# Delta rule's recurrence with heads in pairs on 128 partitions and block diagonal states

## The chip, the cores and the metric

One core of a Trainium2 chip runs the kernel. The metric is the device time of one execution in microseconds (us), the median of some runs. The engines: PE (TensorE: matmul; PEld is its load of weights), DVE (VectorE), ACT (ScalarE), POOL (GpSimd), SP (SyncE, which issues DMAs). All data are fp32, and a matmul of fp32 leaves two records in the trace, a transposition one.

## What is computed

Two layers of a first block (attention, gated MLP, convolution, feed-forward on 512 tokens and 256 context tokens), and one layer of a second block. The change touches only the second block's delta rule: 6 heads of 64 columns, 512 tokens in 8 chunks of C = 64. The reference of that part:

```python
def gated_delta_rule(q, k, v, beta, g):
    ...
    L = jnp.where(strict, jnp.einsum('bhncd,bhnsd->bhncs', k_beta, k) * decay, 0.0)
    A = jnp.eye(C, dtype=f32) + L
    u = lax.linalg.triangular_solve(A, v * beta[..., None], left_side=True, lower=True, unit_diagonal=True)
    w = lax.linalg.triangular_solve(A, k_beta * jnp.exp(gc)[..., None], left_side=True, lower=True, unit_diagonal=True)
    qk = jnp.einsum('bhncd,bhnsd->bhncs', q, k) * decay
    q_dec = q * jnp.exp(gc)[..., None]
    k_dec = k * jnp.exp(gc[..., -1:] - gc)[..., None]
    g_last = jnp.exp(gc[..., -1])

    def step(S, xs):
        u_i, w_i, qk_i, qd_i, kd_i, gl_i = xs
        v_new = u_i - jnp.einsum('bhcd,bhde->bhce', w_i, S)
        o = jnp.einsum('bhcd,bhde->bhce', qd_i, S) + jnp.einsum('bhcs,bhse->bhce', qk_i, v_new)
        S = S * gl_i[..., None, None] + jnp.einsum('bhcd,bhce->bhde', kd_i, v_new)
        return S, o
```

Behind it stand a sparse attention of 6 heads, a pooling branch, an output projection and a feed-forward layer.

## The kernel before

The program is written out by hand for each engine: `second_pe`, `second_act`, `second_dve` and `second_pool` are the instruction streams of the second block, and semaphores (`signal`, `.at`, `wait_ge`, `then_inc`) order them. Each engine works its stream in program order. `Chain` orders dependent instructions on one engine: `link` waits for the instruction itself, `note` only counts it, `meet` waits for all counted so far. `bank(b, n, at)` is a slice of one of the eight banks of PSUM. `turn` is a transposition by PE. In `pe.matmul(out, a, b)` the first operand a is the stationary one: the trace writes its rows\*columns first (64\*64) and then the moving operand's or the output's shape. Where an operand has 64 partitions, PE works in half of its rows; where the output has 64 partitions, in half of its columns.

Tokens lie in four tiles of 128 (i = 0..3), so a tile holds two chunks: an even one in the partitions 0 to 63, an odd one in 64 to 127 (the slice r). A unit u is three heads of one tile, so there are 8 units. The stages, in order of time:

- Stage A (L1004 to L1007, evictions L831): `heads_cm(g)` turns q and k, one head at a time, from token-major to channel-major, [64 partitions, 512 tokens]: 12 groups of 4 transpositions into `qT` and `kT`, through four banks.
- Decay products (L1009 to L1023): for each of 24 heads and tiles, four matmuls of 128\*128 (L1017, L1018) form exponents, and two of 64\*128 (L1020, L1021) form k k' and k q'. ScalarE takes six exponentials per unit, VectorE multiplies (L1320, L1323).
- Transpositions of L (L1025), then VectorE forms the first inverses (L1335), and a third group of `heads_cm` turns the decayed q (L1032): 6 groups of 4.
- Inverse levels (L1035 to L1073): 5 levels of 8 units, with ScalarE and VectorE; the second form of the inverse is had by a transposition.
- w and u products (L1077 to L1088): per head one matmul of 128\*64 (L1084, w, channel-major in 64 partitions) and one of 128\*128 with 64 moving columns (L1086, u). ScalarE evicts w into `kT`, VectorE u into `qkv2` (L1371). Then VectorE clears `state` (L1373).
- Recurrence (PE L1092 to L1111, ACT L883, DVE L1374 to L1386), 8 chunks one after another. PE waits for the state (s_s_up), multiplies it by w (L1097, 6 matmuls), VectorE subtracts from u (L1379), PE forms for each head the state's increment (L1105), q times state (L1107) and the intra-chunk part (L1109), all 64\*64 with 64 moving columns. Then VectorE scales the state (L1382), adds the increment (L1384), and adds the two parts of the output (L1386), after ScalarE has evicted q times state.
- Behind the recurrence: 13 groups of transpositions for the sparse attention (L1116), VectorE's additions (L1397), a matmul with loaded weights (L1129).

Beside the recurrence GpSimd multiplies gains into the attention's q and k (L776 to L783) once the w and u products are done.

## Time and profile before

| | us |
|---|---|
| median of 3 runs | 4323.83 |
| lowest, highest | 4321.07, 4327.37 |
| the profiled execution | 4320.28 |
| its span | 4318.3 |

The profiled execution's clock was on average 0.964 of full speed. The page's busy times are shares of the whole span. The table of stages gives for each stretch the span, the busy time and number of records of each engine, and behind them PEclk, the granted clock of TensorE: 1.00 is 2.4 GHz, 0.50 is 1.2 GHz. In the chain each line is the piece that the end of the program goes back to: start, length, what. In a timeline a line with xN holds N records in a row; its length runs from the first one's start to the last one's end, and the bracket gives the idle time before it and who ended it. Records on PE overlap: the distance from one start to the next tells the pace.

### The profile page before, as it was taken

What the parts mean: (1) busy time and instruction counts of PE and PEld (TensorE: products, weight loads), DVE (VectorE), ACT (ScalarE), POOL (GpSimd) and SP (SyncE); (2) the same over time, 40 slices, a digit from 0 to 9 for tenths busy, and PEclk for the clock granted to TensorE, in tenths of its full rate; (3) what the DMA queues carried; (4) which work ended last, traced back from release to release, by engine and by line L of the source; (5) the groups of instructions that cost most, each with busy time, mean ns of one, the idle gap of its engine ahead of it and who ended that gap; (6) DMA issues with size and microseconds to landing.
All of it is one profiled execution on the core that took longest, in us unless ns stands there. A gap on an engine that the chain in (4) does not pass through costs nothing.

```text
span 4318.3 us, 36448 instructions
## 1 busy us (share of the span) xinstructions
PE 4046.4 (94%) x13693; PEld 2274.7 (53%) x13693; DVE 2026.2 (47%) x3719; ACT 884.8 (20%) x1767; POOL 389.8 (9%) x252
## 2 busy tenths in 40 slices
PE   6999989999998999998998999989998968599999
PEld 3344555555554554544445444446664457556665
DVE  2030530898013456565324099136666135455666
ACT  2111520000123111113133000221112044242111
POOL 1110000254121000000000034110000000000000
PEclk8999999999999999999999999999999989599999
DMA  5552001111112111111110222222222200102222
GB/s 210 195 196 76 2 5 59 59 39 59 39 39 83 44 59 59 59 59 61 59 59 5 72 71 72 78 88 80 96 78 75 73 24 12 49 1 78 98 78 78
DMA packets 124950, 294.51 MB, mean 68 GB/s; under 512 B 5130, under 2 KB 13370, under 8 KB 124800
## 3 DMA queue, kind: packets, MB, share of 16 engines
q1 hardware_dynamic: 107824, 236.58, 15.5%
q0 software_dynamic: 16976, 55.84, 3.8%
q8 instruction: 105, 1.72, 0.2%
q14 instruction: 45, 0.37, 0.0%
HBM read 290.23 MB, written 2.18 MB: 68 GB/s over the span
## 4 chain that ended last, share of the span: by engine, by line
PE 87%; DVE 6%; ACT 3%; DMA 2%; issue 1%; POOL 0%; DVEq 0%; SPq 0%; ACTq 0%
PE psum L357 30%; PE psum L1944 30%; PE psum L2003 14%; PE psum L1938 3%; PE psum L2048 2%; DMA sb_rc<-in_ada_b 1%; PE psum L2031 1%; ACT sb_rc L1703 1%; PE psum L1989 1%; DMA sb_ring<-in_ada_w 1%; PE psum L1043 1%; ACT sb_rb L1703 1%; PE psum L1063 1%; PE psum L2032 1%; ACT sb_ht L1703 0%
## 5 line engine op out<-in xcount | busy, mean ns | idle before, releaser
L1944 PE MATMUL psum<-sb_ht,sb_ring 128*128 128x512 f32 (+1 forms) x2448 | 891.7, 526 | 3.7 <-DVE sb_kvt L2331 2.1
L1944 PEld LDWEIGHTS psum<-sb_ht,sb_ring 128*128 128x128 f32 x2448 | 464.0, 190 | 431.2 <-issue 409.8
L2319 DVE SCALAR_TENSOR_TENSOR sb_rc<-sb_rc,sb_vec x960 | 475.6, 573 | 0.0
L2003 PE MATMUL psum<-sb_ring,sb_ht 128*128 128x512 f32 (+1 forms) x1088 | 464.4, 588 | 5.1 <-DVE sb_rc L2363 3.5
L1703 ACT ACTIVATE sb_rc<-psum 128x512 f32<-128x512 f32 (+2 forms) x330 | 167.1, 524 | 1160.4 <-DVE sb_ra L519 308.1
L357 PE MATMUL psum<-sb_ring,sb_rc 128*128 128x512 f32 x868 | 391.8, 593 | 7.5 <-DVE sb_rc L503 7.5
L2003 PEld LDWEIGHTS psum<-sb_ring,sb_ht 128*128 128x128 f32 x1088 | 207.6, 192 | 260.9 <-issue 255.7
L357 PE MATMUL psum<-sb_ht,sb_ring 128*128 128x256 f32 (+1 forms) x1152 | 305.9, 415 | 0.0
L1703 ACT ACTIVATE sb_kvt<-psum 128x512 f32<-128x512 f32 (+2 forms) x197 | 99.8, 533 | 950.4 <-PE psum L1944 788.1
L1944 PE MATMUL psum<-sb_rc,sb_ring 128*128 128x512 f32 (+1 forms) x768 | 276.6, 522 | 4.3 <-ACT sb_rc L1703 2.5
L357 PEld LDWEIGHTS psum<-sb_ring,sb_rc 128*128 128x128 f32 x868 | 164.5, 190 | 216.6 <-issue 204.2
L357 PE MATMUL psum<-sb_rb,sb_rc 128*128 128x512 f32 x588 | 268.3, 592 | 0.0
L357 PEld LDWEIGHTS psum<-sb_ht,sb_ring 128*128 128x128 f32 x1152 | 219.7, 191 | 71.5 <-issue 0.9
L1703 ACT ACTIVATE sb_rc<-sb_rc 128x512 f32<-128x512 f32 (+3 forms) x232 | 143.1, 686 | 536.0 <-DVE sb_rc L488 526.2
L1944 PEld LDWEIGHTS psum<-sb_rc,sb_ring 128*128 128x128 f32 x768 | 145.6, 190 | 134.8 <-issue 124.5
L357 PE MATMUL psum<-sb_kvt,sb_rc 128*128 128x256 f32 (+1 forms) x672 | 189.0, 426 | 9.4 <-DVE sb_kvt L438 9.4
L1938 PE MATMUL psum<-sb_ident,sb_rb 128*128 128x128 f32 (+3 forms) x748 | 116.4, 298 | 83.0 <-ACT sb_rb L1703 18.7
L357 PEld LDWEIGHTS psum<-sb_rb,sb_rc 128*128 128x128 f32 x588 | 111.7, 190 | 133.2 <-issue 130.6
L1663 POOL TENSOR_TENSOR sb_rb<-sb_kvt 128x768 f32<-128x768 f32 (+1 forms) x16 | 127.5, 7980 | 441.1 <-ACT sb_kvt L1703 441.1
L357 PEld LDWEIGHTS psum<-sb_kvt,sb_rc 128*128 128x128 f32 x672 | 130.6, 195 | 59.5 <-issue 20.9
L1938 PEld LDWEIGHTS psum<-sb_ident,sb_rb 128*128 128x128 f32 (+3 forms) x748 | 88.8, 149 | 126.4 <-issue 49.6
L2003 PE MATMUL psum<-sb_ring,sb_rb 128*128 128x512 f32 x320 | 140.5, 600 | 8.2 <-issue 8.2
(355 smaller groups left out, 4399.9 us busy)
## 6 DMA issues: line engine op xcount, KB each, us to landing
sb_ring<-in_w_in SPq DMA_DIRECT2D x37, 2048.0 KB, 7.9
sb_ring<-in_w_ff SPq DMA_DIRECT2D x32, 2048.0 KB, 7.9
sb_rc<-in_ada_w POOLq DMA_DIRECT2D x20, 2048.0 KB, 8.3
sb_ring<-in_w_ffn SPq DMA_DIRECT2D x16, 2048.0 KB, 7.9
sb_ring<-in_w_out SPq DMA_DIRECT2D x6, 2048.0 KB, 8.0
sb_ring<-in_ada_w SPq DMA_DIRECT2D x4, 2048.0 KB, 12.8
sb_ring<-in_w_gmlp_o SPq DMA_DIRECT2D x4, 2048.0 KB, 8.3
sb_ring<-in_w_attn_o SPq DMA_DIRECT2D x4, 2048.0 KB, 8.0
```

The lines of the kernel that those rows point to most:

```text
L357: last = pe.matmul(bank(to, width), left[k], right[k], start=k == 0, stop=k == depth - 1)
L1043: last = pe.matmul(bank(u % 2, P, h * P), bt[:, u % 4, h, :], xi[:, u, h, :], start=True, stop=True)
L1063: last = pe.matmul(bank(2 + u % 3, P, h * P), lm[:, u, h, :], xit[:, u, h, :], start=True, stop=True)
L1663: pool.tensor_tensor(acc[:, j, 0:n * P], o, g, ALU.mult).then_inc(s_merged.sem, 1)
L1703: return act.activation(out_, in_, f, **kw)
L1938: return pe.transpose(out_, in_, ident[0:k, 0:k])
L1944: last = pe.matmul(bank(b + v, m), ring[:, slot, k, j * P:(j + 1) * P], rhs[:, k, a:a + m], start=k == 0, stop=k == KT - 1)
L1989: last = pe.matmul(out_[32 * q:32 * q + 32, :], ccol[:, k, :], w[:, k, :], start=half == 0, stop=half == 1)
L2003: last = pe.matmul(bank(4 + g % 4, width), lhs[:, k, i * P:(i + 1) * P], ring[:, slot, k, 0:width], start=k == 0, stop=k == KT - 1)
L2031: pe.matmul(bank(2 * (u % 2)), q, key[:, 0:TOK], start=True, stop=True)
L2048: last = pe.matmul(bank(6 + o % 2, m), kv[:, kt_, v0:v0 + HD], PT[:, k, 0:m], start=k == 0, stop=k == len(tiles) - 1)
L2319: step = stt(conv_slot(j, a, m), conv_slot(j + 1, a + k, m), vec[:, j, k:k + 1], conv_slot(j, a, m), op0=ALU.mult, op1=ALU.add)
```

## The change

Heads go in pairs. `qT` and `kT` are [128 partitions, 3 pairs, 512 tokens]: the even head in the lower 64 partitions, the odd one in the upper. `heads_cm` turns 128 columns at a time, so the 12 and 6 groups become 6 and 3. The decay products take a head's half (`one_head`), and a head's k k' and k q' stand side by side in one of two banks by the head's parity, so VectorE multiplies them by six instructions per unit instead of four. The w and u products go by tile (6 heads, 4 rounds of evictions instead of 8), w into the half of its head. `state` is [128, 3, 128]: for each pair a block diagonal matrix, whose other blocks stay zero. The product with w and q times state become 3 matmuls of 128\*64 with 128 moving columns each, the increment 3 of 64\*128 into a whole pair (the blocks off the diagonal aren't used); the intra-chunk part stays at 6 of 64\*64. The order in a chunk changes: q times state now comes before the wait for the new v; the increment and the output signal apart (s_kv_ps, s_o2_ps); VectorE scales the state in two halves after q times state is read, adds in two halves after the increment, and only then waits for the output's parts; ScalarE evicts on s_qs_ps.

```diff
-        qT = hflat[0:D2, 0:3072].rearrange("p (h n) -> p h n", h=H2)
-        kT = hflat[0:D2, 3072:6144].rearrange("p (h n) -> p h n", h=H2)
+        HP = H2 // 2
+        qT = hflat[:, 0:HP * TOK].rearrange("p (g n) -> p g n", g=HP)
+        kT = hflat[:, HP * TOK:2 * HP * TOK].rearrange("p (g n) -> p g n", g=HP)
+
+        def one_head(ap, h, i):
+            return ap[D2 * (h % 2):D2 * (h % 2) + D2, h // 2, i * P:(i + 1) * P]
...
-        state = cstate[0:D2, :]
+        state = cstate[:, :].rearrange("p (g d) -> p g d", g=HP)
...
-            pool.wait_ge(*s_wu_ps.at(0, 8))
+            pool.wait_ge(*s_wu_ps.at(0, MT))
...
-                act.wait_ge(*s_o2_ps.at(0, c + 1))
+                act.wait_ge(*s_qs_ps.at(0, c + 1))
                 fn(qkv2[r, i, 0:384], bank(1 + c % 2, 384)[r, :]).then_inc(s_o2_sb.sem, 1)
...
-                at = (0, 384, 0)[g // 6] + (g % 6) * D2
+                at = (0, 384, 0)[g // HP] + (g % HP) * P
                 for i in range(MT):
-                    last = turn(bank(g % 4, P, i * P)[0:D2, :], qkv2[:, i, at:at + D2])
+                    last = turn(bank(g % 4, P, i * P), qkv2[:, i, at:at + P])
...
-                    k_ = kT[:, h0 + h, i * P:(i + 1) * P]
-                    pe.matmul(bank(b0 + 2, P, h * P), k_, k_, start=True, stop=True)
-                    last = pe.matmul(bank(b0 + 3, P, h * P), k_, qT[:, h0 + h, i * P:(i + 1) * P],
+                    k_ = one_head(kT, h0 + h, i)
+                    pe.matmul(bank(b0 + 2 + h % 2, P, 256 * (h // 2)), k_, k_, start=True, stop=True)
+                    last = pe.matmul(bank(b0 + 2 + h % 2, P, 256 * (h // 2) + P), k_, one_head(qT, h0 + h, i),
                                      start=True, stop=True)
...
+            for i in range(MT):
+                if i >= 2:
+                    pe.wait_ge(*s_w_sb.at(0, i - 1))
+                    pe.wait_ge(*s_u_sb.at(0, i - 1))
+                for h in range(H2):
+                    at, u = h * D2, 2 * i + h // 3
+                    pe.matmul(bank(2 * (i % 2), P, h // 2 * P)[D2 * (h % 2):D2 * (h % 2) + D2, :],
+                              kbe[:, i, at:at + D2], xit[:, u, h % 3, :], start=True, stop=True)
+                    last = pe.matmul(bank(2 * (i % 2) + 1, D2, at), xit[:, u, h % 3, :],
                                      qkv2[:, i, 768 + at:768 + at + D2], start=True, stop=True)
                 last.then_inc(s_wu_ps.sem, 1)
...
                 pe.wait_ge(*s_s_up.at(0, c + 1))
-                for h in range(H2):
-                    last = pe.matmul(bank(0, D2, h * D2)[r, :], kT[:, h, col], state[:, h * D2:(h + 1) * D2],
-                                     start=True, stop=True)
+                for g in range(HP):
+                    last = pe.matmul(bank(0, P, g * P)[r, :], kT[:, g, col], state[:, g, :], start=True, stop=True)
                 last.then_inc(s_vs_ps.sem, 1)
-                pe.wait_ge(*s_vn.at(0, c + 1))
                 if c >= 2:
                     pe.wait_ge(*s_oi_sb.at(0, c - 1))
+                for g in range(HP):
+                    last = pe.matmul(bank(1 + c % 2, P, g * P)[r, :], qT[:, g, col], state[:, g, :],
+                                     start=True, stop=True)
+                last.then_inc(s_qs_ps.sem, 1)
+                pe.wait_ge(*s_vn.at(0, c + 1))
+                for g in range(HP):
+                    last = pe.matmul(bank(3, P, g * P), kdec[r, i, g * P:(g + 1) * P],
+                                     qkv2[r, i, 768 + g * P:768 + (g + 1) * P], start=True, stop=True)
+                last.then_inc(s_kv_ps.sem, 1)
                 for h in range(H2):
...
+                    last = pe.matmul(bank(4 + c % 2, D2, h * D2)[r, :], qkt[r, 2 * i + h // 3, h % 3, r0:r0 + CH2],
+                                     qkv2[r, i, 768 + h * D2:768 + (h + 1) * D2], start=True, stop=True)
                 last.then_inc(s_o2_ps.sem, 1)
...
                 for h in range(3):
                     at = 6 * i + h0 + h
...
+                    ch.note(stt(lm[:, u, h, :], bank(b, P, at_), small[:, BETA, at:at + 1], lm[:, u, h, :],
+                                op0=ALU.mult, op1=ALU.mult))
+                    last = tt(qkt[:, u, h, :], bank(b, P, at_ + P), qkt[:, u, h, :], ALU.mult)
+                last.then_inc(s_lq.sem, 1)
...
+                copy(qkv2[:, i, 768:1152], bank(2 * (i % 2) + 1, 384)).then_inc(s_u_sb.sem, 1)
+            dve.wait_ge(*s_u_sb.at(0, MT))
+            dve.memset(cstate[:, :], 0.0).then_inc(s_s_up.sem, 1)
...
                 tt(v_, v_, bank(0, 384)[r, :], ALU.subtract).then_inc(s_vn.sem, 1)
+                dve.wait_ge(*s_qs_ps.at(0, c + 1))
+                dve.wait_ge(*s_s_up.at(0, c + 1))
+                halves = [(slice(D2 * e, D2 * e + D2), slice(6 * i + e, 6 * i + 6, 2)) for e in range(2)]
+                for q, heads in halves:
+                    ch.note(tt(state[q, :, q], state[q, :, q], bc(glast[q, c % 2, heads], D2), ALU.mult))
+                dve.wait_ge(*s_kv_ps.at(0, c + 1))
+                ch.meet()
+                for q, heads in halves:
+                    last = tt(state[q, :, q], state[q, :, q], bank(3, 384).rearrange("p (g d) -> p g d", g=HP)[q, :, q],
+                              ALU.add)
+                last.then_inc(s_s_up.sem, 1)
+                dve.wait_ge(*s_o2_sb.at(0, c + 1))
                 dve.wait_ge(*s_o2_ps.at(0, c + 1))
...
                 tt(qkv2[r, i, 0:384], qkv2[r, i, 0:384], bank(4 + c % 2, 384)[r, :], ALU.add).then_inc(s_oi_sb.sem, 1)
```

## Rows read from the trace of the kernel before

**Rows 1.** The page, first section: busy time of each engine.

```profile
PE 4046.4 (94%) x13693; PEld 2274.7 (53%) x13693; DVE 2026.2 (47%) x3719; ACT 884.8 (20%) x1767; POOL 389.8 (9%) x252
```

**Rows 2.** Busy time by stage; behind POOL stand PEclk, DMA share, GB/s.

```profile
3500.60:3509.50 8.90, 7.99 (x48) 6.83 (x48) 6.43 (x13) 6.42 (x12) 0.00 (x0) 0.70 0.00 0
...
3650.00:3667.30 17.30, 17.22 (x96) 11.54 (x94) 4.49 (x13) 3.43 (x8) 6.04 (x12) 1.00 0.00 0
...
3669.70:3673.90 4.20, 4.10 (x36) 3.91 (x36) 0.04 (x1) 0.13 (x1) 4.20 (x7) 0.51 0.01 4
3674.90:3718.10 43.20, 29.29 (x336) 26.66 (x336) 15.79 (x30) 3.39 (x7) 1.50 (x3) 0.50 0.00 1
...
3777.00:3799.00 22.00, 20.43 (x98) 10.81 (x100) 16.89 (x64) 11.67 (x46) 0.00 (x0) 0.50 0.01 1
```

**Rows 3.** Chain in order of time, recurrence: start us, us, what.

```profile
3675.12 1.55 PE psum L1097 x12
...
3676.69 0.57 DVE sb_rb L1379
...
3678.91 0.56 DVE sb_cstate L1382
...
3680.10 1.55 PE psum L1097 x12
...
3687.60 1.55 PE psum L1097 x12
...
3718.14 1.98 PE psum L1938 x8
```

**Rows 4.** Timeline, stage A: start us, us, what, idle time before it.

```profile
3506.03 3.49 ACT L1703 ACTIVATE sb_ht<-psum 64x512 f32<-64x512 f32 x7 [0.26 <-PE psum L1938]
...
3509.57 0.49 PE L1017 MATMUL psum<-sb_x 128*128 128x128 f32 x2 [0.91 <-ACT sb_ht L1703]
```

**Rows 5.** Timeline of PE, shapes in turn in the sparse attention.

```profile
3782.77 0.69 PE L1938 MATMUL psum<-sb_ident,sb_rb 128*128 128x128 f32 x2
3783.39 0.70 PE L1186 MATMUL psum<-sb_rb,sb_rc 128*64 128x128 f32 x4
```

**Rows 6.** Timeline of PE, one head of the decay products.

```profile
3516.47 0.49 PE L1017 MATMUL psum<-sb_x 128*128 128x128 f32 x2
3516.80 0.39 PE L1018 MATMUL psum<-sb_x,sb_ident 128*128 128x128 f32 x2
3517.02 0.39 PE L1017 MATMUL psum<-sb_x 128*128 128x128 f32 x2
...
3518.20 0.49 PE L1017 MATMUL psum<-sb_x 128*128 128x128 f32 x2
```

**Rows 7.** Timeline, the last unit's multiplications and what follows.

```profile
3552.79 0.87 DVE L1320 SCALAR_TENSOR_TENSOR sb_kvt<-psum,sb_x,sb_kvt 128x128 f32<-128x128 f32 x3 [3.85 <-ACT sb_rc L1703]
3553.58 0.54 DVE L1323 TENSOR_TENSOR sb_rc<-psum,sb_rc 128x384 f32<-128x384 f32 x1
...
3554.18 0.47 PE L1938 MATMUL psum<-sb_ident,sb_kvt 128*128 128x128 f32 x1 [3.11 <-DVE sb_rc L1323]
```

**Rows 8.** Timeline, the third group of transpositions and the first level.

```profile
3577.57 2.10 ACT L1703 ACTIVATE sb_ht<-psum 64x512 f32<-64x512 f32 x4 [0.26 <-PE psum L1938]
...
3580.02 0.35 PE L1043 MATMUL psum<-sb_ra,sb_kvt 128*128 128x128 f32 x1 [1.07 <-ACT sb_ht L1703]
```

**Rows 9.** Timeline, an eviction of u.

```profile
3656.34 0.36 DVE L1251 COPY sb_rb<-psum 128x192 f32<-128x192 f32 x1 [1.82 <-PE psum L1086]
```

**Rows 10.** Timeline, the first chunk's product and subtraction.

```profile
3668.28 0.88 PE L1097 MATMUL psum<-sb_cstate,sb_ht 64*64 64x64 f32 x12 [1.06 <-DVE sb_cstate L1373]
...
3669.19 0.55 DVE L1379 TENSOR_TENSOR sb_rb<-sb_rb,psum 64x384 f32<-64x384 f32 x1 [1.06 <-PE psum L1097]
```

**Rows 11.** Busy time in the recurrence's first 2 us, columns as in rows 2.

```profile
3668.00:3670.00 2.00, 1.09 (x14) 0.98 (x15) 0.67 (x2) 1.83 (x4) 2.00 (x4) 0.95 0.00 0
```

**Rows 12.** Timeline, VectorE's first addition behind the recurrence.

```profile
3720.84 0.57 DVE L1397 TENSOR_TENSOR sb_ra<-sb_kvt,sb_vec 64x248 f32<-64x248 f32 x1 [2.52 <-ACT sb_kvt L1703]
```

More of the change, by code:

```diff
@@ L651, in build_program @@
         s_gs_ps = signal("gs_ps", 1)
-        s_h2_ps = signal("h2_ps", 18, after=s_bg_ps)
-        s_h2_sb = signal("h2_sb", 18, after=s_bo_sb)
+        s_h2_ps = signal("h2_ps", 9, after=s_bg_ps)
+        s_h2_sb = signal("h2_sb", 9, after=s_bo_sb)
         s_dec_ps = signal("dec_ps", 8, after=s_bo_ps)
@@ L665, in build_program @@
         s_xt_ps = signal("xt_ps", 32)
-        s_wu_ps = signal("wu_ps", 8)
-        s_w_sb = signal("w_sb", 8)
-        s_u_sb = signal("u_sb", 8)
+        s_wu_ps = signal("wu_ps", MT)
+        s_w_sb = signal("w_sb", MT)
+        s_u_sb = signal("u_sb", MT)
         s_vs_ps = signal("vs_ps", 8)
         s_vn = signal("vn", 8)
+        s_qs_ps = signal("qs_ps", 8)
+        s_kv_ps = signal("kv_ps", 8)
         s_o2_ps = signal("o2_ps", 8)
@@ L827, in heads_out @@
                 act.wait_ge(*s_h2_ps.at(0, g + 1))
-                dst = (qT, kT, qT)[g // 6][:, g % 6, :]
-                fn(dst, bank(g % 4)[0:D2, :]).then_inc(s_h2_sb.sem, 1)
-            for g in range(12):
+                fn((qT, kT, qT)[g // HP][:, g % HP, :], bank(g % 4)).then_inc(s_h2_sb.sem, 1)
+            for g in range(2 * HP):
                 heads_out(g)
@@ L848, in second_act @@
             fn(nss, nss, ACT.Sqrt, scale=1.0 / D2, bias=eps[:, 0:1]).then_inc(s_nsa_rt.sem, 1)
-            for g in range(12, 18):
+            for g in range(2 * HP, 3 * HP):
                 heads_out(g)
@@ L873, in second_act @@
             level_evictions(4, True)
-            for u in range(8):
-                i, h0 = u // 2, 3 * (u % 2)
-                act.wait_ge(*s_wu_ps.at(0, u + 1))
-                fn(kT[:, h0:h0 + 3, i * P:(i + 1) * P],
-                       bank(2 * (u % 2), 384)[0:D2, :].rearrange("p (h n) -> p h n", h=3)).then_inc(s_w_sb.sem, 1)
+            for i in range(MT):
+                act.wait_ge(*s_wu_ps.at(0, i + 1))
+                fn(kT[:, :, i * P:(i + 1) * P],
+                   bank(2 * (i % 2), 384).rearrange("p (g n) -> p g n", g=HP)).then_inc(s_w_sb.sem, 1)
             for i in range(MT):
@@ L1031, in second_pe @@
             pe.wait_ge(*s_lt_sb.at(0, 8))
-            for g in range(12, 18):
+            for g in range(2 * HP, 3 * HP):
                 heads_cm(g)
-            pe.wait_ge(*s_h2_sb.at(0, 18))
+            pe.wait_ge(*s_h2_sb.at(0, 3 * HP))
             def level_products(level, last_level):
@@ L1076, in second_pe @@
             pe.wait_ge(*s_vb2.at(0, 1))
[L1077 to L1086 removed]
+            for i in range(MT):
+                if i >= 2:
[6 more added lines that the diff above has]
+                    last = pe.matmul(bank(2 * (i % 2) + 1, D2, at), xit[:, u, h % 3, :],
                                      qkv2[:, i, 768 + at:768 + at + D2], start=True, stop=True)
                 last.then_inc(s_wu_ps.sem, 1)
[L1090 to L1091 removed]
+            pe.wait_ge(*s_w_sb.at(0, MT))
+            pe.wait_ge(*s_u_sb.at(0, MT))
             for c in range(NCH):
@@ L1367, in second_dve @@
             dve.reciprocal(nrs, nss).then_inc(s_nsa_rs.sem, 1)
-            for u in range(8):
-                i, h0 = u // 2, 3 * (u % 2)
-                dve.wait_ge(*s_wu_ps.at(0, u + 1))
-                copy(qkv2[:, i, 768 + h0 * D2:768 + (h0 + 3) * D2], bank(2 * (u % 2) + 1, 192)).then_inc(s_u_sb.sem, 1)
-            dve.wait_ge(*s_u_sb.at(0, 8))
-            dve.memset(state[:, :], 0.0).then_inc(s_s_up.sem, 1)
+            for i in range(MT):
+                dve.wait_ge(*s_wu_ps.at(0, i + 1))
+                copy(qkv2[:, i, 768:1152], bank(2 * (i % 2) + 1, 384)).then_inc(s_u_sb.sem, 1)
+            dve.wait_ge(*s_u_sb.at(0, MT))
+            dve.memset(cstate[:, :], 0.0).then_inc(s_s_up.sem, 1)
             for c in range(NCH):
```

35 lines of the change are left out of this document (4 added, 31 removed).

## The prediction

> **What bounds the kernel now.** I read the page's first section first: TensorE (PE) is busy for 94% of the span [rows 1]. That is an average over three layers, of which the change touches only one stretch of the last, some 218 us long. So the second view is the table of busy times by stage [rows 2]; the reader should see that PE is busy for nearly all of the w and u products (17.22 of 17.30 us) and for 68% of the recurrence (29.29 of 43.20), and that the granted clock is 1.00 (2.4 GHz) in the first and 0.50 (1.2 GHz) in the second. The third view is the chain in order of time [rows 3]: it shows which step ends last in each chunk. An even chunk (3680.10 to 3687.60) takes 7.50 us: 1.55 us for the product with the state, 0.57 for the subtraction, some 4.1 for 36 PE records, then two state updates of 0.56 [rows 2, 3]. An odd chunk (3675.12 to 3680.10) takes 4.98, because its three kinds of product lie in three different quarters of the array and run at the same time: 36 records between 3677.30 (the subtraction's end and 0.04) and 3678.91, 1.6 us instead of 4.1. Nothing is hidden in this stage: every us taken off a chunk is taken off the end.
>
> **Stage A, q and k to channel-major.** Before: 12 groups of 4 transpositions. ScalarE's evictions take 0.59 and wait 0.26 for PE, so they come 0.85 apart and PE is the pace, at 0.213 us a transposition; the last seven go from 3506.03 to 3509.52, and the decays start at 3509.57 [rows 4]. After: 6 groups of 4, of 128 columns instead of 64. What a 128-column transposition costs lies between 0.213 and 0.31 (two took 0.62 with a change of shape [rows 5]); I take 0.213, since what moves is 128 columns in both. An eviction is 512 elements a partition in both, 0.59. So the sixth eviction starts where it starts now, 3506.03, ends at 3506.62, and PE goes on at 3506.67: **2.9 us less**. Bounds: 3.5, if the clock is up earlier, to 0.6, at 0.31 each (4 x 0.31 x 5 = 6.2 instead of 4.3 to the sixth eviction, and 0.4 for the first).
>
> **Decay products.** 24 heads of 12 records of PE. One head takes 1.725 us (3516.47 to 3518.20), the same records and shapes after; only the partitions of k and q alternate between the lower and upper half [rows 6]. Between equal shapes two records take 0.22 (3516.80 to 3517.02), so 12 would take 1.33: the two changes of shape (128\*128 to 64\*128 and back) cost the other 0.39, **0.2 us for each change at the full clock**. VectorE per unit: today three of 128x128 (0.87) and one of 128x384 (0.54), then six of 128x128, some 0.28 apart, 1.7 us. It waits 3.85 us before each unit's, so this is covered; only the last unit's tail is bare, since the transpositions wait for it [rows 7]: **0.3 us more**. A move to the other half of the partitions could cost nothing (in odd chunks moves between quarters cost nothing [rows 3]) or up to a change of shape; I take nothing.
>
> **Third group (decayed q).** Six evictions become three: now the third starts at 3577.57 and would end at 3578.16; the sixth ends at 3579.67 and PE starts the levels at 3580.02 [rows 8]. **1.5 us less**; the low end is 0.5, if the clock comes up later because PE has less work there and the first level runs at 1.2 GHz.
>
> **w and u products.** The same 96 records, in 17.3 us; each head changes shape twice (17.3 / 48, 0.36 us from one pair of records to the next) and does so after too. The evictions are fewer but larger; the last one lies bare before the state is cleared: VectorE's 192 elements take 0.36, 384 take 0.55 [rows 9, 10]: **0.2 us more**. GpSimd's wait ends with the same last product; what it does then is nearly over by 3674.9 (1.50 us are left [rows 2]) and is waited for only behind the recurrence.
>
> **Recurrence.** A product in fp32 leaves two records of MATMUL in the trace. Per chunk PE has 48 of them today (12 and 36, all 64\*64) and 30 after: 6 for v (128\*64, 128 columns), 6 for q times state, 6 for the state's increment (64\*128), 12 for the intra-chunk part (64\*64, 64 columns). At the **full clock**: 6 records of 128 columns are 6 x 0.111 = 0.67, three times, 2.0; 12 of 64 columns go from 0.72 to 0.88 (12 took 0.88 with fill [rows 10]). Changes of shape: three per chunk at 0.2. PE: 2.0 + 0.7 + 0.6 = **3.3 us a chunk**. The dependent chain of the same chunk: v product 0.67 + 0.22 fill, subtraction 0.57 and wake-up 0.04 [rows 3], increment 0.89, two additions of 192 elements 0.63 (0.36 each by the copy of as many [rows 9], starting 0.27 apart), wake-up 0.06: 3.08. PE is late by a little; the decays (0.63) start when q times state is read, about 1.5, and end before the increment (2.4). So the addition of the output and ScalarE's eviction are covered. Eight chunks, the last with its fill and the output's addition: 7 x 3.3 + 4.0 = 27.1, against 3668.28 to 3718.14, 49.9 [rows 3, 10]: **22.8 us less**. Bounds: 3.1 a chunk (a gain of 24.4) and 4.2 (15.6, a change of shape at 0.5). At the **half clock**: 6 x 0.213 three times, 3.84; 12 x 0.11, 1.4; a change at 0.2 to 0.3 (two transpositions of 0.213 that take 0.62 when they stand between other shapes [rows 5]), 0.7: 5.9 a chunk, 7 x 5.9 + 6.7 = 48.0, **a gain of only 1.9**.
>
> **Which clock.** This is the largest term, and I chose as follows. The w and u products, with as many changes of shape as work, kept 1.00 for 17 us; PE then idled 1.1 us, worked 0.88, idled 0.6, and the clock fell (0.95 in 3668 to 3670, then 0.50) and stayed down though PE worked 4.1 us on end with 64\*64 [rows 2, 10, 11]. After, PE idles once, 1.3 us, and then has v and q products on all 128 rows without a pause, 1.3 us, and nearly no wait from there on. In stage A transpositions on all 128 rows brought the clock up (0.70 over a stretch that began at 0.50) [rows 2]. Against it: 3777 to 3799, PE busy 20.4 of 22 us with mixed shapes, at 0.50 [rows 2]. But that stage had to rise, the recurrence has only to stay up, and half its work is on 128 rows. I take the full clock.
>
> **What follows it.** The next transpositions now run at 1.2 GHz: from 3718.14 to the start of the addition at 3720.84 are 2.7 us, with 8 x 0.213 of PE in it; at the full clock 0.85 less [rows 3, 12]. **0.8 us less.**
>
> The Trainium skill has two rules that bear on this. Its page "TensorEngine Tiling (Array Packing)", section "Key Properties", says that a change of the tiling mode, not of the tile, drains TensorE. That speaks against the change, which brings three modes into a chunk that had one; the trace agrees with 0.2 us a change, and by it the sum is the one above. Its page "TensorE: Matmul & The Clock Gate", Part 1, lets sustained busy time alone release the throttle; by that even a recurrence that began at 1.2 GHz would soon run at 2.4, and the half-clock case would be one of two slow chunks, 2 x 2.6 more than the forecast, 4301.5. The trace doesn't agree for 64\*64 products, which worked 4.1 us on end and stayed at 0.50 [rows 2].
>
> **The sum.** 2.9 - 0.3 + 1.5 - 0.2 + 22.8 + 0.8 = 27.5. The profiled execution took 4320.3 (span 4318.3), the median of the runs is 4323.8; 4292.8 for the one, **4296.3 for the median**, which I predict.
>
> **Rivals.** (1) The clock falls as it does now and stays at 1.2 GHz: 1.9 + 2.9 - 0.3 + 1.5 - 0.2 = 5.8, 4318.0, no change to be told. For it speaks the same fall at the same place now, and 3777 to 3799. If it comes back halfway, 4 x 2.6 = 10.4 more than the forecast, 4306.7. (2) Changes of shape cost 0.5 between a half-height and a full-height tile, or VectorE's output addition delays the next subtraction (it ends at 3.9 of a chunk, the next v product at 3.3 + 0.9 = 4.2, so 0.3 are left): 4.2 a chunk, 7.2 us more, 4303.5. (3) Slower: each move to the other half of the array costs like a change of shape plus a weight load that isn't pulled ahead, 0.2 + 0.19, at 24 heads of the decays and 24 of w and u: 18.7 us more, beside the half clock: 4336.7. It is slower from 0.12 us a move on (5.8 / 48), measurably from 0.3; at the full clock it would still be faster. Against it: moves between quarters are free in odd chunks. (4) The change does nothing, because another engine covers the recurrence: excluded, since in each chunk the chain goes through PE and VectorE alone.
>
> **How the numbers follow.** Forecast (4290 to 4302) 0.69; rival 2, 0.10; rival 1, 0.12 for the whole stage and 0.05 with a late return; slower 0.04. Some 0.2%, 8.6 us, is what a measurement of this kernel can tell from no change. Faster: 0.69 + 0.10 + 0.05 = 0.84, same 0.12, slower 0.04. Rival 1 for the whole stage, the slower case and a little of the forecast stay outside; low end: 3.1 a chunk and 2 us of clock elsewhere, 4290; high end 4314.
>
> **What would show it.** Granted clock 1.00 through the recurrence, a distance of 3.3 us from one v product to the next, equal in even and odd chunks; 24 transpositions and six evictions before the decays; a head of the decays still at 1.73 us, w and u at 17.3. Wrong if a chunk takes 5.9 at 0.50, or a head of either product stage grows.

## The result, and the profile after

| | before | after |
|---|---|---|
| median (5 runs each) | 4323.83 | 4299.59 |
| lowest, highest | 4320.71, 4327.47 | 4297.97, 4300.66 |
| span of the profiled execution | 4318.3 | 4296.6 |

The ratio is 0.9943, interval 0.9928 to 0.9957: 24.2 us less, where 27.5 were forecast (the two profiled executions lie 21.9 apart, and the stages below are read from them). TensorE is still the engine that is nearly always busy (compare [rows 1]):

```profile
PE 4040.1 (94%) x13513; PEld 2266.0 (53%) x13513; DVE 2031.1 (47%) x3747; ACT 879.5 (20%) x1754; POOL 390.0 (9%) x252
```

The kernel after, busy time by stage (columns as in [rows 2]): stage A, third group, inverse levels, w and u products, recurrence.

```profile
3502.73:3508.79 6.06, 5.37 (x24) 4.97 (x24) 5.82 (x11) 3.62 (x7) 0.00 (x0) 0.57 0.00 0
3574.16:3577.96 3.80, 2.79 (x12) 2.42 (x13) 1.96 (x4) 1.79 (x3) 0.00 (x0) 0.50 0.00 0
3577.96:3649.80 71.84, 69.39 (x577) 66.90 (x577) 39.14 (x77) 35.37 (x72) 0.00 (x0) 0.96 0.00 0
3649.80:3668.59 18.79, 17.53 (x96) 11.74 (x97) 4.95 (x10) 2.70 (x6) 7.16 (x14) 0.99 0.00 1
3668.59:3697.93 29.34, 27.57 (x240) 23.68 (x241) 21.45 (x48) 5.23 (x11) 7.96 (x11) 0.95 0.01 1
```

And the same stages of the kernel before, w and u (18.59, 1.00) left out:

```profile
3500.66:3509.57 8.91, 7.99 (x49) 6.84 (x49) 6.41 (x12) 6.47 (x13) 0.00 (x0) 0.70 0.00 0
3574.80:3580.02 5.22, 4.15 (x24) 3.44 (x25) 1.96 (x4) 3.28 (x6) 0.00 (x0) 0.73 0.00 0
3580.02:3649.69 69.67, 67.18 (x577) 64.54 (x577) 39.15 (x77) 35.32 (x72) 0.00 (x0) 1.00 0.00 0
...
3668.28:3718.14 49.86, 34.26 (x384) 31.30 (x384) 17.27 (x32) 5.42 (x11) 8.12 (x12) 0.52 0.00 1
```

Read line against line: stage A -2.85, third group -1.4, **levels +2.2** (at 0.96 instead of 1.00), w and u +0.2, recurrence -20.5 (PEclk 0.95 instead of 0.52). Everything ahead of stage A, which the change doesn't touch, took 2.1 us longer in this execution; in executions of other kernels with the same code there, stage A began anywhere from 3499.4 to 3506.9, so nothing here shows it to be an effect of the change.

The recurrence on PE, first chunk and a later one, of the kernel after (start us, us; the distance of two starts tells the pace):

```profile
3668.59 1.51 PE L1100 MATMUL psum<-sb_cstate,sb_ht 128*64 128x128 f32 x6 [1.26 <-DVE sb_cstate L1378]
3669.90 1.49 PE L1105 MATMUL psum<-sb_cstate,sb_ht 128*64 128x128 f32 x6
3671.32 1.15 PE L1110 MATMUL psum<-sb_rb,sb_kvt 64*128 64x128 f32 x6
3672.40 0.91 PE L1114 MATMUL psum<-sb_rb,sb_rc 64*64 64x64 f32 x12
3674.03 0.87 PE L1100 MATMUL psum<-sb_cstate,sb_ht 128*64 128x128 f32 x6 [0.73 <-DVE sb_cstate L1393]
...
3684.16 0.87 PE L1100 MATMUL psum<-sb_cstate,sb_ht 128*64 128x128 f32 x6
3684.86 0.82 PE L1105 MATMUL psum<-sb_cstate,sb_ht 128*64 128x128 f32 x6
3685.67 0.93 PE L1110 MATMUL psum<-sb_rb,sb_kvt 64*128 64x128 f32 x6
3686.53 0.91 PE L1114 MATMUL psum<-sb_rb,sb_rc 64*64 64x64 f32 x12
3687.41 0.87 PE L1100 MATMUL psum<-sb_cstate,sb_ht 128*64 128x128 f32 x6
```

From 3684.16 to 3687.41 are 3.25 us, with no gap; all of chunks 3 to 7 take 3.25 or 3.26, even and odd alike, and the chain goes through PE alone:

```profile
3680.92 0.84 PE psum L1100 x6
3681.76 0.66 PE psum L1105 x6
3682.42 0.93 PE psum L1110 x6
3683.35 0.84 PE psum L1114 x12
```

This answers [rows 3], where each product waited for VectorE and ran at half the clock. The first chunk took 5.44, the second 3.61, the last 4.01. Two things are late in the first: the clock, and VectorE's scaling of the state (L1389), which takes 1.73, then 1.17, and from then on 0.74. VectorE of the kernel after:

```profile
3671.42 1.73 DVE L1389 TENSOR_TENSOR sb_cstate<-sb_cstate,sb_glast 64x192 f32<-64x192 f32 x2 [0.73 <-PE psum L1105]
...
3675.59 1.17 DVE L1389 TENSOR_TENSOR sb_cstate<-sb_cstate,sb_glast 64x192 f32<-64x192 f32 x2
...
3679.20 0.74 DVE L1389 TENSOR_TENSOR sb_cstate<-sb_cstate,sb_glast 64x192 f32<-64x192 f32 x2
```

### The profile page after: what moved, and what is told of

It reads as the page before. It is cut to its first block, busy times and chain, and to the rows that moved or that the text cites. A ratio compares the mean times of both kernels' runs of the same rounds, so it can differ in the third digit from the quotient of the medians.

```text
span 4296.6 us, 36109 instructions
## 1 busy us (share of the span) xinstructions
PE 4040.1 (94%) x13513; PEld 2266.0 (53%) x13513; DVE 2031.1 (47%) x3747; ACT 879.5 (20%) x1754; POOL 390.0 (9%) x252
## 3 DMA queue, kind: packets, MB, share of 16 engines
HBM read 290.23 MB, written 2.18 MB: 68 GB/s over the span
## 4 chain that ended last, share of the span: by engine, by line
PE 87%; DVE 6%; ACT 3%; DMA 2%; issue 1%; POOL 0%; DVEq 0%; SPq 0%
PE psum L357 30%; PE psum L1956 30%; PE psum L2015 14%; PE psum L1950 3%; PE psum L2060 2%; DMA sb_rc<-in_ada_b 1%; PE psum L2043 1%; ACT sb_rc L1715 1%; PE psum L2001 1%; DMA sb_ring<-in_ada_w 1%; PE psum L1047 1%; ACT sb_rb L1715 1%; PE psum L1067 1%; PE psum L2044 1%; ACT sb_ra L1715 0%
## 5 line engine op out<-in xcount | busy, mean ns | idle before, releaser
L1950 PE MATMUL psum<-sb_ident,sb_rb 128*128 128x128 f32 (+2 forms) x712 | 113.0, 300 | 83.3 <-ACT sb_rb L1715 18.9
L1950 PEld LDWEIGHTS psum<-sb_ident,sb_rb 128*128 128x128 f32 (+2 forms) x712 | 86.3, 154 | 125.4 <-issue 48.8
```

The lines of the kernel that those rows point to most:

```text
L1950: return pe.transpose(out_, in_, ident[0:k, 0:k])
```

## Experiments

Four questions: how much of the recurrence's 20.5 us is the clock and how much the structure; what holds the clock; why the first chunks are long; and why the levels took more. "Filling" below means matmuls of the identity by itself into a bank that nobody reads. The kernel before ran beside each group of four: its median was 4323.2 beside the first four rows, 4321.0 beside the next four, 4320.3 beside the last. "GpSimd late" has two executions, the others have four to ten; the recurrence is that of one profiled execution each.

| kernel | median | ratio to before, interval | recurrence us |
|---|---|---|---|
| before, filled | 4316.0 | 0.9987, 0.9977 to 0.9997 | 46.7 |
| after, pause ahead | 4308.1 | 0.9963, 0.9950 to 0.9976 | 30.5 |
| after, q late | 4322.0 | 0.9997, 0.9987 to 1.0007 | 54.7 |
| all by head | 4298.5 | 0.9941, 0.9924 to 0.9959 | 29.7 |
| after, bridge | 4296.7 | 0.9947, 0.9929 to 0.9965 | 28.1 |
| after, q late, bridge | 4303.1 | 0.9972, 0.9957 to 0.9988 | 34.5 |
| by head, bridge | 4297.4 | 0.9946, 0.9928 to 0.9964 | 28.9 |
| by head, warm | 4292.3 | 0.9935, 0.9917 to 0.9953 | 28.7 |
| increment by head | 4296.2 | 0.9945, 0.9930 to 0.9960 | 28.6 |
| GpSimd late | 4297.4 | 0.9946, 0.9927 to 0.9964 | 29.9 |
| turned twice | 4300.4 | 0.9951, 0.9936 to 0.9966 | 29.3 |
| by head, held | 4283.8 | 0.9913, 0.9900 to 0.9927 | 24.0 |

### The structure of before at the full clock

```diff
 # recurrence, kernel before: after the v product / after the 36 products
+                for _ in range(2):
+                    pe.matmul(bank(6, P), ident[:, :], ident[:, :], start=True, stop=True)
...
+                for _ in range(4):
+                    pe.matmul(bank(6, P), ident[:, :], ident[:, :], start=True, stop=True)
```

> The kernel before, with matmuls of ident by ident into an unused bank while PE waits in the recurrence: 2 behind each product with the state, 4 behind each chunk's last product (0.22 us each at 2.4 GHz). Nothing else differs; the output is the same. Theory 1 (most of the 20.5 us came from the clock, not from the fewer products): the clock stays or comes up to 2.4 GHz, an even chunk falls from 7.5 to some 5.1 us, an odd one from 5.0 to 3.7, the recurrence from 49.9 to about 35, the kernel by 15 (4309). Theory 2 (it came from the pairs and the new order, the clock follows): even at 2.4 GHz a chunk stays at 6 or more and the recurrence above 46 us.

Measured: the clock rose, but only halfway through. The kernel before, filled, chunks 1 to 4 and 5 to 8:

```profile
3667.66:3696.08 28.42, 28.42 (x241) 25.77 (x241) 8.66 (x16) 3.48 (x7) 8.15 (x12) 0.52 0.01 1
3696.08:3714.38 18.30, 17.12 (x242) 15.06 (x241) 8.64 (x16) 1.94 (x4) 0.00 (x0) 0.99 0.01 2
```

At 1.00 its chunks took 5.19, 3.72, 5.08 and 4.31, as theory 1 has it; the recurrence still took 46.7 us, since the first four ran at 0.52, although PE was busy without a pause (28.42 of 28.42 us). Eight of them would be about 4 x (5.1 + 3.7) + 0.6 = 36 us (0.6 for the end of the last one), some 14 less than before and some 7 more than after. Counted this way, about **two thirds of the recurrence's gain is the clock, one third the structure** (products and order together). This is an estimate, since no run had the old structure at 1.00 throughout.

### A pause ahead, and q times state behind the wait

```diff
 # pause ahead, VectorE, behind the clearing of the state
+            for _ in range(16):
+                ch.link(dve.memset(cstate[:, :], 0.0))
 # q late, PE
+                pe.wait_ge(*s_vn.at(0, c + 1))
                 for g in range(HP):
                     last = pe.matmul(bank(1 + c % 2, P, g * P)[r, :], qT[:, g, col], state[:, g, :],
...
-                pe.wait_ge(*s_vn.at(0, c + 1))
```

> The changed kernel with 16 more clears of the state before the recurrence, about 6.5 us in which PE idles, so that the clock is at 1.2 GHz when the recurrence starts. Theory 1 (products on all 128 rows bring the clock up by themselves): the first one or two chunks take 5.4 to 5.9 us, the rest 3.26; the recurrence lasts 29 to 33 us, the kernel gains 6.5 to 9 over the changed one's 4299.6. Theory 2 (it was full only because the w and u products came right before): it stays at 1.2 GHz, 5.9 a chunk, 48 us, some 4325.

> The changed kernel with q times state moved back behind the wait for the new v, ahead of the increment. Theory 1 (the order is worth what it hides, 0.66 us of PE under the subtraction): a chunk goes from 3.26 to 3.9 or 4.0 us, the recurrence from 29.3 to 35, the kernel to 4305. Rival: PE idles more in each chunk and the clock falls: 6.5 us a chunk, 52 us, 4322.

After the pause (PE idles 9.67 us instead of 1.26) the recurrence starts at 1.2 GHz, and comes up by itself. The kernel with the pause, chunk 1, chunk 2, chunks 3 to 8:

```profile
3680.14:3685.90 5.76, 5.76 (x30) 5.09 (x30) 1.96 (x5) 0.48 (x1) 0.00 (x0) 0.50 0.00 0
3685.90:3690.39 4.49, 4.49 (x31) 3.93 (x30) 2.51 (x6) 0.49 (x1) 0.00 (x0) 0.70 0.02 4
3690.39:3710.67 20.28, 19.56 (x182) 16.77 (x181) 15.64 (x37) 2.91 (x6) 0.00 (x0) 1.00 0.01 1
```

The first line is also the price of a whole chunk at 1.2 GHz: 5.76, where 5.9 was worked out. Eight of them and some 0.9 for the end of the last are 47 us, only some 3 less than before the change. So counted at the low clock the structure alone is worth 3 us and the clock the rest: what each is worth depends on which is changed first. With q late it doesn't come up at all:

```profile
3670.54:3725.26 54.72, 48.30 (x241) 39.82 (x241) 20.89 (x48) 5.22 (x11) 7.85 (x11) 0.50 0.00 1
```

Same products, same shapes, but PE now stands still 0.74 us in each chunk, and a chunk takes 6.75: the recurrence is 4.9 us longer than before the change, and the whole gain is gone. Rival 1 of the prediction was real; one wait in another place brings it about.

### Bridges: the clock up at the start

```diff
 # ahead of the recurrence, PE, behind the last w and u products
+            for _ in range(6):
+                pe.matmul(bank(6, P), ident[:, :], ident[:, :], start=True, stop=True)
```

> The changed kernel with the same 6 matmuls in the gap before the first chunk. Theory 1 (the first chunk's 5.44 us instead of 3.3 is the clock, which fell at its start): chunk one 3.4 us, the recurrence 27.0 instead of 29.3, the kernel some 2 us less, 4297.5. Rival (the first chunk is slow because VectorE's scaling meets GpSimd, 1.05 us instead of 0.36): 4.5 us or more in spite of the clock, 28.5.

> The changed kernel with q times state behind the wait for the new v (6.75 us a chunk at 1.2 GHz without more), and the 6 matmuls in the gap. Theory 1 (the order's own worth is the 0.66 us that it hides, and the rest of what its move cost was the clock, which never came up): 1.00 throughout, 3.9 to 4.1 us a chunk, 32.5 us, the kernel 4303. Rival (with PE idle behind each v product the clock can't be held, so the order itself carries it): it falls in the first chunks, 6.7 a chunk, 53 us, 4321.

Recurrence of the kernel after with the bridge:

```profile
3667.18:3695.28 28.10, 26.12 (x241) 22.35 (x240) 21.50 (x48) 5.18 (x11) 8.05 (x11) 1.00 0.01 1
```

and with q late and the bridge:

```profile
3667.15:3701.62 34.47, 27.19 (x241) 22.14 (x241) 20.98 (x48) 5.18 (x11) 7.93 (x11) 1.00 0.00 1
```

The position of q times state is worth 34.47 - 28.10 = 6.4 us at the full clock (4.11 us a chunk instead of 3.25), and 25 us where the clock hangs on it. Beside the estimate of 36 us for the old structure at the full clock, that leaves only some 2 us for the pairs themselves (36 against 34.5, in which GpSimd has 0.8); the kernel before with nothing but the new order was not run, so this is an estimate too. Seven of the ten executions with q late and the bridge took 4298.7 to 4306.3, three took 4319.8 to 4324.1, at a mean clock of 0.963 to 0.966 against 0.969 to 0.972; that fits a recurrence at 1.2 GHz, but none of the three was traced. With the bridge alone the first two chunks were 3.84 and 3.99 at the full clock, where later ones take 3.25, so the clock isn't all of their excess. The recurrence took 28.1 where 27.0 was expected, for the same reason.

### Why the first chunks are long

```diff
 # GpSimd, ahead of its gains
-            pool.wait_ge(*s_wu_ps.at(0, MT))
+            pool.wait_ge(*s_qs_ps.at(0, 5))
```

> The changed kernel with GpSimd's gains held back until the fifth chunk's q times state is there, so that it stands still in chunks 1 to 4 and works beside VectorE in chunks 5 to 8. My theory: VectorE's scaling of the state, whose operands both lie in SBUF, is slow because GpSimd reads SBUF at the same time. Then the scaling takes 0.74 in chunks 1 to 4 (now 1.73 in the first, 1.17 in the second), the first two chunks are 0.3 to 1.0 us shorter together (what the clock costs in the first chunk stays), and in chunks 5 and 6 the scaling takes 1.1 to 1.7 and the chunk is 0.3 to 0.7 longer than 3.25; the kernel stays within 1 us. The rival: the first chunk's long scaling comes from something else (TensorE at 1.2 GHz, a first access to the state); then it stays at 1.7 and 1.2, and chunks 5 to 8 stay at 3.25.

GpSimd's gains now run beside chunks 5 to 7, and the long scaling moved with them. VectorE of this kernel, chunks 1, 4, 5, 6 and 7:

```profile
3670.42 0.73 DVE L1389 TENSOR_TENSOR sb_cstate<-sb_cstate,sb_glast 64x192 f32<-64x192 f32 x2 [0.73 <-PE psum L1105]
...
3680.34 0.73 DVE L1389 TENSOR_TENSOR sb_cstate<-sb_cstate,sb_glast 64x192 f32<-64x192 f32 x2
...
3683.60 1.43 DVE L1389 TENSOR_TENSOR sb_cstate<-sb_cstate,sb_glast 64x192 f32<-64x192 f32 x2
...
3687.47 1.19 DVE L1389 TENSOR_TENSOR sb_cstate<-sb_cstate,sb_glast 64x192 f32<-64x192 f32 x2
...
3691.09 1.54 DVE L1389 TENSOR_TENSOR sb_cstate<-sb_cstate,sb_glast 64x192 f32<-64x192 f32 x2
```

The chunks were 4.68, 3.26, 3.25, 3.26, then 3.87, 3.62, 3.98, and 4.01. So GpSimd cost 0.76 in the first chunk and 0.35 in the second, and 4.68 - 3.25 = 1.4 is the clock. TensorE's clock doesn't lengthen the scaling: after the pause, at 1.2 GHz and with GpSimd done, it took 0.74. GpSimd slows only this operation of VectorE; the additions that read PSUM (L1393, L1398) stayed at 0.72 and 0.55 beside it.

The single records show how. Each line above is two instructions. GpSimd's first one in this kernel:

```profile
3683.71 1.10 POOL L784 TENSOR_TENSOR sb_rc<-sb_rc,sb_rope 128x384 f32<-128x384 f32 x1 [26.42 <-PE psum L1105]
```

In chunk 5 the first part of the scaling starts at 3683.60, ahead of this instruction, which runs to 3684.81, and takes its usual 0.35; the second part starts at 3683.98, during it, takes 1.05 and ends at 3685.03. In the traces of the kernel after and of its variants there are 40 such slowed scalings, and each ends 0.21 to 0.22 us behind the end of the GpSimd instruction that was running when it started. So a scaling waits for a GpSimd instruction that is already under way, and isn't just slower beside it.

### All products by head: 64\*64 in four quarters

```diff
 # PE; the increment and q times state in the same manner
-                for g in range(HP):
-                    last = pe.matmul(bank(0, P, g * P)[r, :], kT[:, g, col], state[:, g, :], start=True, stop=True)
+                for h in range(H2):
+                    q = slice(D2 * (h % 2), D2 * (h % 2) + D2)
+                    last = pe.matmul(bank(6 + h % 2, D2, h // 2 * D2)[r, :], kT[q, h // 2, col], state[q, h // 2, q],
+                                     start=True, stop=True)
```

> The changed kernel with all products of the recurrence by head and 64*64, even and odd heads in different halves of the rows (v, q) or of the columns (increment), into different banks where the rows differ; order and signals as changed, the output is the same. Theory 1 (two quarters work at the same time, and no change of shape is left): PE needs 1.8 us a chunk, the chain bounds: 0.6 + 0.6 + 0.6 + 0.7 = 2.5 us at 2.4 GHz, the recurrence 21 us, the kernel 4292. Rival (64-row products don't hold the clock, as in the kernel before): 1.2 GHz, 3.4 to 3.6 us a chunk, 28 us, 4299. Second rival (block diagonal matmuls were what paid, since quarters don't overlap): 3.9 us or more at either clock, 4305.

> The kernel with all products of the recurrence by head (the one before in this study, 3.48 us a chunk at 1.2 GHz), and 6 more matmuls of ident by ident (1.3 us at 2.4 GHz) into an unused bank, which fill PE's idle time between the w and u products and the first chunk. Theory 1 (it ran slow only because the clock fell in that gap and 64-row products don't bring it up; once up, they hold it): 1.00 through the recurrence, 2.5 to 2.7 us a chunk, 21.5 us, the kernel 8 us less than without, 4290. Rival (64-row products don't hold it either): it falls after a chunk or two, 3.3 to 3.5 us a chunk, 28 us, 4298.

Without a bridge, the recurrence by head:

```profile
3670.07:3699.77 29.70, 27.54 (x384) 25.47 (x384) 21.33 (x48) 5.21 (x11) 8.08 (x11) 0.50 0.01 2
```

It runs at 1.2 GHz from end to end and is nearly as fast as the block diagonal form at 2.4: 3.48 us a chunk against 3.25, and this rival's forecast held. The first 12 records of a chunk (v) take 0.69 us to the start of the next group (q), where the kernel before took 1.55 at the same clock: two run at a time. The 48 records never change shape. (VectorE's subtraction and ScalarE's eviction read from two banks here.) With the bridge, chunk 1, chunk 2, chunks 3 to 8:

```profile
3671.67:3674.92 3.25, 2.18 (x50) 1.90 (x49) 2.46 (x6) 1.66 (x4) 3.25 (x5) 1.00 0.02 5
3674.92:3678.68 3.76, 2.18 (x48) 1.90 (x49) 3.49 (x7) 0.49 (x1) 3.76 (x6) 0.89 0.00 0
3678.68:3700.53 21.85, 20.09 (x288) 18.77 (x288) 15.34 (x37) 2.91 (x6) 1.05 (x2) 0.50 0.01 2
```

It began at 1.00, PE was busy for 2.18 us of a chunk, and the clock fell in the second.

### The increment alone by head

```diff
 # PE
-                for g in range(HP):
-                    last = pe.matmul(bank(3, P, g * P), kdec[r, i, g * P:(g + 1) * P],
-                                     qkv2[r, i, 768 + g * P:768 + (g + 1) * P], start=True, stop=True)
+                for h in range(H2):
+                    q = slice(D2 * (h % 2), D2 * (h % 2) + D2)
+                    last = pe.matmul(bank(3, D2, h * D2)[q, :], kdec[r, i, h * D2:(h + 1) * D2],
+                                     qkv2[r, i, 768 + h * D2:768 + (h + 1) * D2], start=True, stop=True)
```

> The changed kernel with only the state's increment by head: six products of 64*64 into the two diagonal blocks, in place of three of 64*128 whose other blocks aren't used. A chunk then changes shape twice instead of three times (the increment has the shape of the output part), and two quarters could work at once. My theory: the shape change (0.2) and the side-by-side work (the increment took 0.93) save 0.3 to 0.4 a chunk: 2.85 to 2.95 us instead of 3.25, the recurrence 26.5 to 27 instead of 29.3, the kernel some 2.5 us less than the changed one, if the clock stays at 2.4 GHz. The rival: VectorE's chain (worked out at 3.08 a chunk) or the lack of overlap between products that read the same half of the rows leaves 3.1 to 3.3 a chunk, and the kernel as it is. A second way to go: more products on half of the rows let the clock fall, and the chunks take 4.5 to 5.5.

A chunk of this kernel on PE:

```profile
3677.30 0.87 PE L1100 MATMUL psum<-sb_cstate,sb_ht 128*64 128x128 f32 x6 [0.41 <-DVE sb_cstate L1394]
3678.00 0.82 PE L1105 MATMUL psum<-sb_cstate,sb_ht 128*64 128x128 f32 x6
3678.81 0.56 PE L1111 MATMUL psum<-sb_rb,sb_kvt 64*64 64x64 f32 x12
3679.22 0.86 PE L1115 MATMUL psum<-sb_rb,sb_rc 64*64 64x64 f32 x12
3680.47 0.87 PE L1100 MATMUL psum<-sb_cstate,sb_ht 128*64 128x128 f32 x6 [0.39 <-DVE sb_cstate L1394]
```

The increment's step fell from 0.86 to 0.4, yet the chunk only from 3.25 to 3.17: PE now waits 0.4 for VectorE. What is next is not the chain the prediction named (v, subtraction, increment, additions), but q times state, scaling, additions: 0.70 and 0.81 for the two products, 0.05 to the scaling (3678.86), 0.84 to the additions (3679.70), 0.72 for them and 0.05 to the next product, 3.17. The expected 2.85 to 2.95 was wrong: it left the scaling out of the chain; the rival's 3.1 to 3.3 held.

### The levels' 2.2 us

```diff
 # PE (ScalarE and the counts alike): 12 groups instead of 6, 6 instead of 3
-            for g in range(2 * HP):
+            for g in range(12):
...
-            for g in range(2 * HP, 3 * HP):
+            for g in range(12, 18):
```

> The changed kernel with every group of transpositions of stage A and of the third group done twice, with its eviction (12 and 6 groups again, as before the change, but of 128 columns). It undoes the gain of both and leaves the rest of the change. My theory: the first inverse level took 2.2 us longer after the change because TensorE had less work in the third group and the clock rose only at 3583.1; with six groups it rises before the levels. Stage A 8.9 instead of 6.1 (+2.9), third group 5.2 instead of 3.8 (+1.4), levels 69.7 instead of 71.8 (-2.2), recurrence unchanged: the kernel 2.1 us above the changed one. The rival: the levels' 2.2 us come from another part of the change (where the operands lie, the banks); they stay at 71.8, and the kernel is 4.3 us above the changed one.

Stage A, third group and levels of this kernel:

```profile
3501.58:3510.44 8.86, 7.85 (x49) 7.62 (x49) 6.42 (x12) 6.56 (x13) 0.00 (x0) 0.72 0.00 0
3575.80:3582.13 6.33, 5.35 (x24) 4.98 (x25) 1.96 (x4) 3.58 (x6) 0.00 (x0) 0.54 0.00 0
3582.13:3651.84 69.71, 67.19 (x576) 64.55 (x577) 39.19 (x77) 35.31 (x72) 0.00 (x0) 1.00 0.00 1
```

The levels are back at 69.7: their cost was the clock's, not the change's operands or banks. The third group itself took 6.3, not 5.2: it ran at 0.54, since the clock rose only at its end. So the two stages together take 76.0 us here, 75.6 in the kernel after and 74.9 in the kernel before: the larger third group doesn't earn its cost back. Why the clock came up later than in the kernel before, with as many transpositions, stays open. With stage A the three stages are 3.2 us longer than after, where 2.1 was expected.

### The clock held through everything

```diff
 # stage A and third group, PE, while it waits for other engines: fillings
+            for _ in range(12):
+                pe.matmul(bank(7, P), ident[:, :], ident[:, :], start=True, stop=True)
 # per chunk, behind the output part, into two unused banks
+                for h in range(8):
+                    q = slice(D2 * (h % 2), D2 * (h % 2) + D2)
+                    pe.matmul(bank(5 * (h % 2), D2)[r, :], kT[q, 0, col], ident[q, 0:D2], start=True, stop=True)
```

The output part stays in one bank here, so that another is free for the extra products. The first kernel below has the fillings ahead of stage A and the third group and the bridge; the second has the extra products per chunk too, and 14 fillings behind the recurrence. Both are by head.

> The by-head kernel with the bridge, and with two more fillings by matmuls of ident by ident while PE waits for VectorE: 12 before the first transpositions of q and k, 9 before the third group. Theory 1 (these stages and the first inverse level are slow by the clock alone): stage A takes 4.2 instead of 6.1 us, the third group 2.3 instead of 3.8, the levels 69.6 instead of 71.8: 5.6 us less than with the bridge alone, 4285. Rival (ScalarE's evictions of 0.59 bound stage A, and the level's first products wait for VectorE): at most 2 us less.

> The kernel with all the recurrence's products by head (64*64), with the two fillings that keep TensorE busy before the recurrence, and in addition, in every chunk, eight extra 64*64 products into two unused banks behind the output part, and 14 transposition-like fillings ahead of the matmul that waits for the loaded weights behind the recurrence. All of the reference is still computed. My theory: it is how long TensorE stands still in a chunk, and not the height of the tiles, that lets the clock fall; with the pauses filled it stays at 2.4 GHz (granted 1.00 from 3668 to the end of the recurrence), a chunk of the later six takes 2.5 to 2.7 us instead of 3.48, the first two 3.2 to 3.8 because of GpSimd, the recurrence some 22 us instead of 28.9, and the kernel comes to some 4290. The rival: products on half of the rows don't hold the clock whatever their number; it falls within the first chunks as before, a chunk takes 3.5 to 3.9 (the extra products then cost up to 0.4 each chunk), the recurrence 29 to 31 us, the kernel 4297 to 4300.

By head, warm: stage A 3.9, third group 2.6, levels 69.7, and the kernel 5.1 us less than with the bridge alone (5.6 expected), but the clock fell in the recurrence as without them (0.62 on average). By head, held, stage A, third group, levels and recurrence:

```profile
3501.93:3505.72 3.79, 2.84 (x25) 2.60 (x25) 3.65 (x7) 3.08 (x7) 0.00 (x0) 1.00 0.00 0
3571.11:3574.13 3.02, 1.99 (x13) 1.78 (x13) 1.96 (x4) 1.58 (x3) 0.00 (x0) 0.83 0.00 0
3574.13:3643.85 69.72, 67.18 (x576) 64.54 (x577) 39.19 (x77) 35.31 (x72) 0.00 (x0) 1.00 0.00 0
...
3662.71:3686.69 23.98, 20.11 (x514) 18.61 (x513) 20.93 (x48) 5.05 (x11) 8.04 (x11) 1.00 0.01 3
```

1.00 to the end, with nothing but 64\*64 products in the recurrence. Chunks took 3.24 and 3.75 beside GpSimd, then 2.69 and 2.82 in turn, where 2.5 to 2.7 was expected (24.0 us in all instead of 22); VectorE is now busy for 20.93 of 23.98 us. The matmul with loaded weights behind it took 7.13 us instead of 9.44. At 4283.8 us this kernel is faster than both, and its ratio's interval (up to 0.9927) ends just below that of the kernel after (from 0.9928). That products on half of the rows don't hold the full clock whatever their number, which the run with the bridge suggested, is refuted. With the extra products PE stood still 0.60 and 1.11 us in the first two chunks, with the bridge alone 1.07 and 1.58. The extra products both shorten the pauses and add work, and no run tells the two apart.

## Why the prediction was right, and where it was off

| step | forecast | measured | |
|---|---|---|---|
| stage A | -2.9 | -2.85 | right, for the reason given |
| decays | +0.3 | +0.1 | right: a head stays at 1.73 |
| third group | -1.5 | -1.4 | right alone, but |
| levels | 0 | +2.2 | missing from the sum |
| w and u | +0.2 | +0.2 | right |
| recurrence | -22.8 | -20.5 | size off |
| what follows | -0.8 | -1.5 | |
| ahead of stage A | 0 | +2.1 | not of the change |

- **Which clock** was the largest choice, and it held, but more narrowly than its chance says. The clock did fall (3668.4), as rival 1 says, and came back at 3671.8 in the first chunk. The runs with the pause and with q late show what carries it: chunks of these shapes without an idle PE bring it up, chunks with 0.74 us of idleness don't, and hold it only in most executions. A busy PE alone isn't enough: the kernel before, filled, was busy for all of its first four chunks, mostly with 64\*64 products, and stayed at 0.50 from 3669.1 to 3696.4. The forecast's argument that the recurrence "has only to stay up" was wrong, since the clock fell while PE still waited for the first chunk; the one on the products of 128 rows without a pause was right.
- **Recurrence**: seven chunks were taken at 3.3. Five were 3.25, as PE's steps of 0.70, 0.81, 0.86 and 0.88 add up; the first two were 9.05 instead of 6.6: 1.4 by the clock, 1.1 by GpSimd. The step that failed is the one on w and u, which asked only who waits for GpSimd, not what it slows. The last chunk was 4.01, forecast 4.0.
- **Levels**: the prediction saw this mechanism, but only as a low end of the third group's gain ("the first level runs at 1.2 GHz", 0.5 instead of 1.5), and mis-sized it. The first level's 18 records took 2.49 us before and 4.18 after (fences below); with the records behind them that is 2.2 us. Third group and levels together are 0.8 us longer than before, though doing the group twice doesn't win that back (76.0 us).
- **What follows**: the next addition starts 1.88 us behind the recurrence's end instead of 2.70, the 0.8 forecast. Another 0.4 is in the matmul with loaded weights (9.44 instead of 9.86), part of which now ran at the full clock. The rest wasn't looked for, and may be no effect: from the recurrence's end to the end of the program, the traces without fillings there took 598.1 to 600.3 us (598.7 after, 600.2 before).
- **Rival 2** (dearer changes of shape): no. The steps that change shape are 0.14 to 0.2 above their own work (0.81 and 0.86 from start to start, for 0.67 each). **Rival 3** (moves to the other half of the array): no. Decays and w and u show nothing for them. Neither the block diagonal zeros nor the taller tiles were needed: by head, the quarters at 1.2 GHz gave 29.7 us.
- The Trainium skill's page "TensorE: Matmul & The Clock Gate", Part 1, has sustained busy time release the throttle. The trace doesn't agree: by head, PE was busy for 27.54 of 29.70 us and stayed at 0.50 throughout, and the kernel before, filled, was busy for 28.42 of 28.42 us at 0.52 in its first four chunks.

In sum the span is 21.7 us shorter, 23.8 without what lies ahead of stage A. Of the 3.7 between that and 27.5, the recurrence has 2.3, the levels 2.2 and the third group 0.1; the decays (0.2) and what follows (0.7) gave back.

The first level, kernel before:

```profile
3580.02 2.49 PE L1043 MATMUL psum<-sb_ra,sb_kvt 128*128 128x128 f32 x18 [1.07 <-ACT sb_ht L1703]
```

Kernel after:

```profile
3577.96 4.18 PE L1047 MATMUL psum<-sb_ra,sb_kvt 128*128 128x128 f32 x18 [1.01 <-ACT sb_ht L1715]
```

## What to carry to other kernels

Where a recurrence is short and dependent, look at the granted clock of its stretch before counting products: a single wait moved behind independent work was worth 6 us by itself and 25 with the clock that hung on it. When a stage ahead of a heavy one gets shorter, ask at which clock the heavy one will now start. Equal small tiles in different quarters can be as fast at 1.2 GHz as a taller form at 2.4, and here eight extra products a chunk, mostly in idle time, held the clock for them (24.0 us instead of 28.7). Where VectorE multiplies two operands from SBUF on the critical path, see what GpSimd has under way.

## What was not expected of the hardware

- **Small products and the clock**: by head, with PE busy 27.54 of 29.70 us, it never rose from 0.50; by head with the extra products, it never fell from 1.00, at 20.11 of 23.98. In the kernel before, filled, 27 us without any pause didn't bring it up, and then it rose and stayed. Whether the extra products could also bring it up from 0.50 wasn't tried.
- **GpSimd and VectorE**: the scaling of 192 elements with both operands in SBUF took 0.35 alone and up to 1.05 beside GpSimd's multiplications, since it waits for the one under way. The kernel before had one scaling beside GpSimd that took its usual 0.55 (3673.93): the GpSimd instruction under way had only 0.14 us left, and the next one took 1.18 instead of 0.86. So GpSimd seems to wait for VectorE as well.
- **Two levels in one kernel**: with q late and the bridge, executions of one program lay in two groups some 20 us apart.
